# Twelve projection blocks of each mixer as plain fp32 products instead of split ones

## The reference

```python
for l in range(DEPTH_2):
    mod = (c_act @ w_ada[l] + b_ada[l]).reshape(B, N_MOD, D_MODEL)
    sh1, sc1, gt1, sh2, sc2, gt2, sh3, sc3, gt3 = [mod[:, i, None, :] for i in range(N_MOD)]
    ...
    hn = rms_norm(h, g_mix[l]) * (1.0 + sc2) + sh2
    proj = hn @ w_mix_in[l]                     # 1024 x 2560
    p_att, p_rwkv, p_conv = jnp.split(proj, [ATT_PROJ_WIDTH, ATT_PROJ_WIDTH + RWKV_PROJ_WIDTH], axis=-1)
    y_att = sliding_window_sink_attention(p_att, ...)
    y_rwkv = rwkv7_time_mix(p_rwkv, ...)
    y_conv = short_conv_mix(p_conv, conv_w[l])
    mixed = jnp.concatenate([y_att, y_rwkv, y_conv], axis=-1) @ w_mix_out[l]
    h = h + (1.0 + gt2) * mixed
```

## Time and profile before

| | us |
|---|---|
| median of 3 runs (lowest, highest) | 2011.97 (2010.78, 2017.2) |
| profiled execution, its own time | 2011.86 |
| its span, first to last instruction | 2009.8 |
| TensorE busy / VectorE / ScalarE in it | 1945.2 / 1167.7 / 756.6 |
| mean granted TensorE clock, share of full | 0.982 |

### The profile page before, as it was taken

How to read it: one execution, slowest core, us unless ns; L and a number is a source line. 1 busy time by engine, 2 the same in 40 slices (tenths; PEclk the granted TensorE clock), 3 DMA queues, 4 the chain that set the end, 5 groups by cost and what they waited for, 6 DMA issues and landing times.

```text
span 2009.8 us, 30515 instructions
## 1 busy us (share of the span) xinstructions
PE 1945.2 (97%) x12668; PEld 1741.4 (87%) x12668; DVE 1167.7 (58%) x1786; ACT 756.6 (38%) x1071; POOL 31.6 (2%) x64
## 2 busy tenths in 40 slices
PE   7999989899999999999999999999999999999998
PEld 6788868688866667999988889999999988889998
DVE  1493152566666655977646448776877447536443
ACT  3222330343444444433443224434443334325442
POOL 6000000000000000000000000000000000000000
PEclk9999999899999999999999899999999999999999
DMA  8344411446799987777531046776676541023441
GB/s 253 105 147 147 143 51 37 189 164 234 260 387 355 392 316 280 273 313 273 167 127 43 22 168 229 284 304 258 242 297 273 168 147 43 22 102 132 187 189 63
DMA packets 124457, 391.08 MB, mean 195 GB/s; under 512 B 11810, under 2 KB 72532, under 8 KB 95008
## 3 DMA queue, kind: packets, MB, share of 16 engines
q1 hardware_dynamic: 122048, 387.19, 52.0%
q0 software_dynamic: 1968, 0.90, 0.2%
q10 hardware_dynamic: 304, 1.06, 0.1%
HBM read 388.06 MB, written 1.05 MB: 194 GB/s over the span
## 4 chain that ended last, share of the span: by engine, by line
PE 90%; DVE 5%; issue 2%; ACT 2%; DMA 0%; SPq 0%; DVEq 0%; ACTq 0%
PE bank L538 89%; PE bank L573 1%; DMA slab<-in_w_up 0%; DVE slab_low L1868 0%; ACT w_hi L1435 0%; DVE hT L1830 0%; DVE tiny L1913 0%; DVE region L2431 0%; DVE hT L1853 0%; DVE region L1912 0%; DVE region L2413 0%; DVE region L1932 0%; ACT region L1344 0%; ACT L1322 0%; ACT lnt L1352 0%
## 5 line engine op out<-in xcount | busy, mean ns | idle before, releaser
L1868 DVE TENSOR_TENSOR slab_low<-slab,w_hi 128x2048 fp32r<-128x2048 f32 x152 | 348.1, 2291 | 183.2 <-ACT w_hi L1435 182.9
L538 PE MATMUL bank<-h_hi,w_hi 128*128 128x256 f32 x1408 | 399.3, 284 | 1.5 <-DVE h_lo L1860 1.5
L538 PE MATMUL bank<-h_lo,w_hi 128*128 128x256 f32 x1408 | 397.4, 282 | 0.0
L538 PE MATMUL bank<-h_hi,slab_low 128*128 128x256 f32 x1408 | 396.6, 282 | 0.0
L1435 ACT ACTIVATE w_hi<-slab 128x2048 fp32r<-128x2048 f32 x152 | 290.4, 1912 | 147.3 <-DMA slab<-in_w_up 78.0
L538 PEld LDWEIGHTS bank<-h_hi,w_hi 128*128 128x128 f32 x1408 | 266.5, 189 | 3.0 <-issue 3.0
L538 PEld LDWEIGHTS bank<-h_hi,slab_low 128*128 128x128 f32 x1408 | 266.3, 189 | 0.0
L538 PEld LDWEIGHTS bank<-h_lo,w_hi 128*128 128x128 f32 x1408 | 265.5, 189 | 0.0
L538 PE MATMUL bank<-gT_hi,d_hi 128*128 128x256 f32 x832 | 234.1, 281 | 0.0
L538 PE MATMUL bank<-gT_hi,d_low 128*128 128x256 f32 x832 | 233.7, 281 | 0.0
L538 PE MATMUL bank<-gT_lo,d_hi 128*128 128x256 f32 x832 | 233.7, 281 | 0.0
(11 more groups left out here) (298 smaller groups left out, 2648.0 us busy)
## 6 DMA issues: line engine op xcount, KB each, us to landing
slab<-in_w_ffn_in SPq DMA_DIRECT2D x88, 1024.0 KB, 8.2
slab<-in_w_up SPq DMA_DIRECT2D x64, 1024.0 KB, 9.0
region<-in_w_ada SPq DMA_DIRECT2D x112, 512.0 KB, 6.6
region<-in_w_ffn_out SPq DMA_DIRECT2D x44, 1024.0 KB, 5.0
region<-in_w_down SPq DMA_DIRECT2D x32, 1024.0 KB, 5.5
slab<-in_w_in SPq DMA_DIRECT2D x23, 1024.0 KB, 5.4
slab<-in_w_mix_in SPq DMA_DIRECT2D x20, 1024.0 KB, 10.2
hT<-in_w_ada SPq DMA_DIRECT2D x32, 512.0 KB, 5.9
```

The costliest lines, as they stand in the source:

```text
L538: return nc.tensor.matmul(o, lhsT, rhs, start=start, stop=True, skip_group_check=True)
L1868: V_.tensor_tensor(slab_low[slot][:, :], slab[slot][:, :], w_hi[h % 3][:, :].bitcast(F), ALU.subtract)\
```

## The change

The twelve blocks become plain products that read `hT` and the slabs directly. Gone are `project_split`, the `mix_hi`, `m_hi` and `m_lo` tiles, and the work of ACT and DVE that filled them. The first two blocks are still paced, in a new function `project_paced`, by `hn`, which DVE counts up for each chunk of `hT`. TensorE now waits itself for a slab to land. Order and number of loads on SP's queue stay the same. The FFNs keep their split.

```diff
-            def project_split(blocks, w_hi, x_hi, x_lo, paced=False):
-                for b in blocks:
-                    if b % 2 == 0:
-                        hi, lo = split_slab(b // 2, w_hi)
...
-                    for kc in range(KD):
-                        mm(ps, hi[:, kc, cols], x_hi[:, kc, :], kc == 0)
-                        mm(ps, hi[:, kc, cols], x_lo[:, kc, :])
-                        m = mm(ps, lo[:, kc, cols], x_hi[:, kc, :])
...
+            def project_paced(nblocks):
+
+                s = arrive().rearrange("p (k c) -> p k c", k=KD)
+                places = [product("act")[:, 0:T] for _ in range(2)]
+                for kc in range(KD):
+                    pe.wait_ge(S["hn"], w("hn"))
+                    for x, ps in enumerate(places):
+                        m = mm(ps, s[:, kc, x * P:(x + 1) * P], hT[:, kc, :], kc == 0)
+                        if kc == KD - 1:
+                            m.then_inc(S["for_act"], 1)
+                used("for_act")
+                project(hT, nblocks - 2, "act")
...
-                    w("hn", KD)
-
-                    project_split(range(12), mix_hi, m_hi, m_lo, paced=True)
+                    project_paced(12)
...
-                for k in range(2):
-                    split_slab(mix_hi, k)
-                norm(parts=m_hi)
+                norm()
                 for b in range(8):
                     evac(V["praw"][:, b, 1:1 + T])
-                    if b % 2 and b < 6:
-                        split_slab(mix_hi, b // 2 + 3)
...
-                if mixer is not None:
-                    for k in range(2):
-                        mix_low(mixer, k)
                 add_output(seg, gate, "down_done", members[-1].u + 1)
...
-                norm(xT, gain(1), hT, bias=shift(1), split=True, hi=m_hi, lo=m_lo)
-                for k in range(2, MIX_SLABS):
-                    mix_low(l, k)
+                norm(xT, gain(1), hT, bias=shift(1))
```

More of the change, by code:

```diff
@@ L139 @@
     "cin_ready": "combine weights within a token's group", "cg_ready": "those of the gathered tokens",
-    "phi_ready": "the high part of a slab of a split projection", "plo_ready": "and its low part",
     "gut": "a step's hidden activations", "ada_step": "one of eight parts of an adaLN chunk added",
@@ L155 @@
 GATHER_BANKS = 6
-STAGE1_SLABS, MIX_SLABS = 0, 6
 @dataclass
@@ L337, in parts_at @@
             return nc.alloc_sbuf_tensor_at(name, [P, *shape], FR, offset=offset)
-        def over(name, view, shape=(SLAB,)):
-            return parts_at(name, shape, region_at + 4 * (view.offset - region[:, 0:1].offset))
         slab_low = [parts_at(f"slab_low{n}", [SLAB], slab_at + 4 * SLAB * n) for n in range(SLOTS)]
@@ L390, in build @@
         B2["th"], B2["yr"] = B2["R"], B2["cs"]
-        mix_hi = [over("mix_hi0", B2["AT"]), over("mix_hi1", B2["Tm"]), over("mix_hi2", B2["csp"])]
-        m_hi = over("m_hi", B2["off"], (KD, T))
-        m_lo = over("m_lo", B2["al"], (KD, T))
         def par_at(name, layer=None):
@@ L480, in build @@
         for_act, for_dve = [], []
-        low_used = []
         up_slab = []
@@ L598, in projection @@
                 return block
[L600 to L606, removed]
-            def project_split(blocks, w_hi, x_hi, x_lo, paced=False):
-                for b in blocks:
-                    if b % 2 == 0:
-                        hi, lo = split_slab(b // 2, w_hi)
-                    if paced and b == 0:
-                        places = [product("act")[:, 0:T] for _ in range(2)]
-                        for kc in range(KD):
-                            pe.wait_ge(S["h_split"], w("h_split"))
-                            for x, ps in enumerate(places):
-                                cols = slice(x * P, (x + 1) * P)
-                                mm(ps, hi[:, kc, cols], x_hi[:, kc, :], kc == 0)
-                                mm(ps, hi[:, kc, cols], x_lo[:, kc, :])
-                                m = mm(ps, lo[:, kc, cols], x_hi[:, kc, :])
[L623 to L636, removed]
@@ L1364, in squares, with norm @@
                         .then_inc(S["sq"], 1)
-            def norm(glu_next=False, parts=None, shift=None):
+            def norm(glu_next=False, shift=None):
                 tables(LNEXP)
@@ L1374, in norm @@
                 else:
-                    split_h(parts)
-                    split_slab(mix_hi, 2)
+                    w("hn", KD)
             def attention(groups, sc, pr, pT, o, mem=False, sink=None):
@@ L1444, in down_high, with split_h @@
                 nc.scalar.activation(d_hi[x][:, :], d_raw[b], ACT.Copy).then_inc(S["dhi_ready"], 1)
[L1446 to L1454, removed]
+            def split_h(shift=None):
                 for j in range(KD):
@@ L1823, in link, with norm @@
                 later()
-            def norm(src, gain, dst, sem="hn", bias=None, split=False, hi=h_hi, lo=h_lo):
+            def norm(src, gain, dst, sem="hn", bias=None, split=False):
                 dve.wait_ge(S["rs"], w("rs"))
@@ L1844, in norm @@
                         dve.wait_ge(S["h_high"], w("h_high"))
-                        V_.tensor_tensor(lo[:, j - 3, :], hT[:, j - 3, :], hi[:, j - 3, :].bitcast(F),
+                        V_.tensor_tensor(h_lo[:, j - 3, :], hT[:, j - 3, :], h_hi[:, j - 3, :].bitcast(F),
                                          ALU.subtract).then_inc(S["h_split"], 1)
@@ L1943, in attend @@
                         probabilities(g - 1)
[L1945 to L1950, removed]
             def ada_piece(seg, p):
@@ L2055, in moe, with ffn @@
                 add_output(0, None, "scattered", N_GROUP - 1)
-            def ffn(seg, gate, chained, mixer=None):
+            def ffn(seg, gate, chained):
                 members = [u for u in UNITS if u.seg == seg]
@@ L2343, in _ @@
                 norm_dense(gain(0), shift(0))
-                ffn(1 + 2 * l, gate(0), False, l)
+                ffn(1 + 2 * l, gate(0), False)
                 modulation(l, (1, 2))
-                norm(xT, gain(1), hT, bias=shift(1), split=True, hi=m_hi, lo=m_lo)
-                for k in range(2, MIX_SLABS):
-                    mix_low(l, k)
+                norm(xT, gain(1), hT, bias=shift(1))
                 link(V_.memset(V["praw"][:, :, 0:1], 0.0))
@@ L2633, in _ @@
                 pool.dma_start(dst, src).then_inc(S["others_in"], 16)
[L2635 to L2643, removed]
 ROW_COUNTS = [sum(n for _, n in ROWS_1), LAYERS * sum(n for _, n in ROWS_2), TAPS * 4, 72, 72,
```

## The result

The changed kernel takes 2017.95 us (median of 12 runs, 2012.05 to 2021.31), the kernel before 2011.24 us (12 runs beside it). The ratio is 1.0034, with a 95% interval of 1.0021 to 1.0047: 6.7 us or 0.34% slower, in the direction and the range forecast, 2.6 us under the forecast time of 2020.6 and just under the 2018 to 2024 us that the prediction held most likely.

What follows compares the result with a forecast made beforehand. TensorE was taken to bound the kernel. Per mixer, 7.2 us of dearer plain products less 2.85 us of waiting and pacing gave +8.7 us over two mixers: 2011.86 + 8.7 = 2020.6 us, range 2014.5 to 2026.5.

Steps and rivals of the forecast that it cites:

- What bounds it: Whole kernel and the twelve blocks: TensorE sets the pace, busy 97% of the span and holding 90% of the chain.
- Price of a block: Twelve blocks on TensorE: a plain block takes 3.457 us against 2.857 split, 0.600 us dearer; 0.432 us a plain product.
- The count of passes: Rival for the twelve blocks: a plain block costs 4/3 of a split one, 3.81 us; +8.6 a mixer, 2029 us; 2%.
- The paced pair: First two blocks: TensorE starts at 991.59 without waiting for `m_lo` and stays ahead-fed by DVE; 2.85 us of waiting and pacing go.
- The sum: Blocks of each mixer: 7.2 us of dearer products less 2.85 us at the start, +4.35 and +4.36, together +8.7 us.
- What goes for nothing: ACT copies and DVE subtractions beside the blocks: removing 22.9 us of ACT and 27.5 us of DVE slab work gains nothing.
- The freed engines: Removed ACT and DVE work priced at nothing; the rival that it would show, giving under 2006 us, had 1%.
- the slabs: Slab loads for the blocks: TensorE waiting for their landing itself was priced at nothing, since loads are issued 15 us ahead.
- After the blocks: Keys, values and all that follows: a shift of 4.35 us goes through whole, but the clock can move a mixer by 7.8 us.
- sign of 166 to 174 us: Profile of the changed kernel: from the keys to the next FFN lie 166 to 174 us, deviating with the granted clock.
- The time: Whole kernel: 2011.86 + 8.7 = 2020.6 us, 0.43% slower; 2018 to 2024 us held at 65%.
- both clock rivals: After the blocks: the clock gives back up to 7.8 us (2012.8, 18%), or takes up to 7.8 more (2028.4, 10%).

Runs made afterwards that it cites:

- ten others plain: Kernel before with the ten blocks behind the paced pair as plain products, the pair still split and paced by `m_lo`: 2018.93 us, ratio 1.0052.
- shift only: Kernel before with ten more products on constants between the twelve split blocks and the keys, nothing else changed: 2018.42 us, ratio 1.0058.

## Why the prediction was right

- **What bounds it.** TensorE held the chain, and still holds it (89%). This was right, and the run with the splitting work left in shows it from the other side: 62 us of work on ACT and DVE are worth 0.1 us in A.
- **Price of a block.** 0.432 us a plain product, from rows outside the mixer; measured in it 44.90 / 104 = 0.4317. Right to a tenth of a per cent. The count of passes (4/3, +17 us) is refuted by the same number.
- **The paced pair.** Start at the end of the constant products, with DVE ahead of TensorE from then on: right. The first product starts 989.17 + 2.59 = 991.76, to the hundredth.
- **The sum.** +4.35 and +4.36 a mixer forecast, +4.32 and +4.33 measured. The decomposition into 7.2 less 2.85 was measured in its parts: +5.96 for ten blocks (6.0 forecast), and the pair -1.42, or -1.6 by difference (4.32 less 5.96) where no wait for `m_lo` follows.
- **What goes for nothing.** The freed engines and the slabs came out as forecast: TensorE shows no DMA wait in the blocks. The shift goes through whole, as forecast: with the mixers filled B is 160.8 us with it and without it.
- **After the blocks.** The prediction saw that equal mixers differed by 7.8 us and put it to the clock, from two rows of granted clock. This was right and shown: with the gaps filled the granted clock is 1.00 and B is 160.8 us in all mixers but one (161.7). It was used only for the width of the range. Its sign of 166 to 174 us from the keys to the next FFN was missed in one mixer: 173.9 us in the second, but 164.6 in the first (161.1 and 3.45 for the keys). The two mixers of before were not the two ends of what the clock does: against the 159.4 us estimated for a mixer without falls, the profile that the forecast started from held some 14 us of falls.
- **The time.** 2020.6 forecast, 2017.95 measured. The 2.6 us between them are not a term of the sum, since A is right to 0.1 us in all. The runs of each of the two kernels lie 9 to 12 us apart, and the interval of the ratio, 4.2 to 9.5 us, holds 8.6. That the time came so close was in part luck: in the profile both clock rivals came true at once, the first mixer gave back 9.3 us and the second took 7.8. Had only one of them come, a right sum would have gone with a time off by about the whole effect.

## What to carry to other kernels

- Splitting fp32 products into three fp32r ones gains only a sixth per block here (2.86 against 3.46 us), and only where the operands' parts are ready in time. Where a chunk-by-chunk producer paced the first products, plain fp32 was the faster form (1.42 us a mixer): it needs neither the high copy nor the subtraction before it may start, and the two products of a chunk (0.86 us) are long enough to hide the next chunk's making (0.66 us). So try a mix of the two forms: plain at the paced start, split behind it.
- In a stretch where TensorE waits often and briefly for other engines, look at the granted clock of equal stretches first. If it differs, fill the waits with products on constants, and read in the trace that each is really shorter than its wait; here this gave 10 us, more than the change under study was about, though two of the fillings cost 1.4 us a mixer.
- Where the clock scatters by more than the effect, size the effect on the stretch that holds it, over both layers, and not on medians: here medians gave 6.1, 6.7 and 9.7 us for the same 8.65.
- The version with both, paced pair plain and all gaps filled, takes 1992.4 us, 0.81% (0.63 to 1.0) less than the kernel before, the lowest median of all tried. Against the same kernel with only the mixers filled (1996.56) it rests on six runs of each.

## What the runs showed of the hardware

- A plain fp32 product of 128 x 128 by 128 x 256 passes in 0.432 us, an fp32r product of the same shape in 0.119 us: 3.63 times, so that one plain product costs 1.21 times the three fp32r ones. What makes up the factor was not separated.
- In the mixers the granted clock fell to half (1.2 GHz) after idle gaps of TensorE of only 0.5 to 1.8 us, and stayed there for 3 to 16 us. The same instruction sequence fell or did not fall from one mixer to the other and from one execution to another, so that B lasted from 161.1 to 170.5 us without filling. A single gap of 1.4 us ahead of the split blocks brought no fall in any profile that has it.
- Three of the profiles (before, ten others plain, shift only) reached the router with falls at the same places to about 0.3 us, other profiles with another pattern. Up to there these kernels run the same instructions. This speaks against falls drawn anew at random in each execution, but three agreeing profiles don't prove it; what sets the pattern is open.
